# The gate of a projected piece: copy and tanh on ScalarE, the product later and in place on VectorE

## The chip, the cores and the metric

The kernel runs on one core of one Trainium2 chip. The metric is the device time of one execution in microseconds (us). Engine names are those of the profile: PE is TensorE's matmul, PEld its weight load, DVE is VectorE, ACT is ScalarE, POOL is GpSimd, SP is SyncE, which issues most DMAs.

## The reference, cut to what matters

A two-layer trunk of width 1024 runs for 1024 prompt tokens and for 8 samples of 4 tokens. Each layer normalizes, projects to 3592 columns, runs four token mixers side by side (S5, HGRN2, mLSTM, retention), gates each, and projects back:

```python
proj = jnp.einsum('bld,de->ble', h, w_in[l]).astype(f32)
...
hq = jax.nn.silu(to_heads(hg_q, HGRN_HEADS))
...
mixed = jnp.concatenate([s5_out * jax.nn.silu(s5_g), hg_out * jax.nn.silu(hg_g),
                         ml_out * jax.nn.silu(ml_g), rt_out * jax.nn.silu(rt_g)], axis=-1)
x = x + jnp.einsum('ble,ed->bld', mixed.astype(x.dtype), w_out[l])
```

The silu of a column g is computed as (tanh(g/2) + 1) * g, and the factor 2 that this leaves is taken out further on. Five of the projected blocks need it: `hg_q`, `hg_g`, the gate columns of `ml_ifg`, `rt_g` and `s5_g`.

## The kernel before, in words

The work runs in four passes n = 0 to 3: two layers, each as a first half of 512 prompt tokens and a second half of 512 prompt tokens with the 32 sample tokens. `make_plan` writes out one list of steps, and each engine walks the whole list in order and does its own part of each step. So the order on every engine is fixed, and an engine that waits holds up all that is behind it in its own queue.

A projection step ("mm", piece) lets PE multiply one piece of a block into one of three PSUM banks, which all pieces, the norm transposes and the out projection use in turn (`PB`, `bank_of`). "tok" blocks give pieces of 128 tokens x 256 columns (32 tokens in four groups of 64 columns for the samples); "ch" blocks (`hg_q`, `s5_g`) give pieces of 128 channels x 512 tokens on even passes and of 256 and 288 tokens on odd ones. Each matmul is done three times, with high and low parts of weights and activations. ACT makes the high part of a weight block (L1132), POOL the low part in eight pieces (L1088). A bank is free for the piece three places on when its `free` semaphore is raised, for which PE waits in `claim`.

The step ("take", piece) comes one piece after its "mm". For a gated piece (kind "av") ACT waits for the full bank and writes tanh(x/2) to one of two halves of the buffer `th` (L1218 and L1219 for "tok" pieces, L1221 for "ch" pieces; L1214 copies eight columns of `ml_ifg` aside first). DVE then multiplies: it reads the tanh from `th` and the piece from PSUM, writes the product to its place in SBUF (L1538 for `hg_q` into `hq`, L1545 for the three "tok" gates, L1548 for `s5_g` into `mixT`) and raises the bank's `free`. ACT's next tanh but one waits for that, since it writes the same half of `th`. `square_sum`, which makes the sums for the norms, uses `th` as scratch.

What lies around these steps, by line:

- L1989 to L2016 on DVE and L1403 to L1418 on ACT prepare one chunk of HGRN2 (steps A0, AX and A1). PE waits for the result at L2477. A0 of a pass's first chunk comes after the last `hg_g` piece.
- L1612, L1625 and L1635 on DVE set up the S5 parameters, woven in between the first pieces of pass 0. PE's L2299 and L2306 and ACT's L1306 and L1308 belong to the same set-up.
- L1904 and L1909 on DVE are the end of S5 of a pass (step z). The takes of the next pass's `hg_g` pieces come right behind it.
- L2402 on PE transposes the eight gate columns of mLSTM. It waits for the `free` of all `ml_ifg` pieces of its pass. ACT's L1380 to L1396 follow it.
- L2195 on DVE ends a chunk of any mixer; L2205 adds an out piece to the residual.

Of the kernel before, what the change touches and what calls it, by code (L numbers as in the profile page):

```python
# [351 lines left out]
def trunk_kernel(nc, inp, out, parts=("hg", "ml", "rt", "s5")):  # L352
    plan = make_plan(parts)
    ctx = ExitStack()
    with ctx:
# [3 lines left out]
        def signal(name, keys, unit=1):  # L359
            return Signal(nc, ctx, name, keys, unit)  # L360
# [249 lines left out]
        ud = nc.dram_tensor("ud", (256, W), F32, kind="Internal").ap()  # L610

        vexp = [QE.rearrange("p l a t -> p (l a t)")[0:TS, 768 + 512 * i:1280 + 512 * i] for i in range(2)]
        gate_of = {"hg": hgate, "rt": rgate, "ml": mgate}
        x1 = nc.dram_tensor("x1", (SEQ + TS, D), F32, kind="Internal").ap()
        x2 = nc.dram_tensor("x2", (SEQ + TS, D), F32, kind="Internal").ap()
# [41 lines left out]
        whi_done = signal("whi_done", in_blocks)  # L657
        wlo_done = signal("wlo_done", [b + (g,) for b in in_blocks for g in range(KT)])
        th_keys = [k for k in pieces if BLOCK[k[1]][4] == "av"]
        th_done = signal("th_done", th_keys)  # L660
        xo_in = [signal(f"xo_in{s}", [k for k in out_pieces if oslot[k] == s], 16) for s in range(3)]
        xo_sum = signal("xo_sum", out_pieces)
        xo_out = [signal(f"xo_out{s}", [k for k in out_pieces if oslot[k] == s], 16) for s in range(3)]
# [73 lines left out]
        def columns(key, lo, hi):  # L737
# [4 lines left out]
            cuts = [(g, max(lo, g * w), min(hi, (g + 1) * w)) for g in range(4)]  # L742
            return [(PB[bank_of[key]].t[TS * g:TS * g + TS, a - g * w:b - g * w], slice(a - lo, b - lo)) for g, a, b in cuts if a < b]

        def before(keys, key, back=1):
            i = keys.index(key)
            return keys[i - back] if i >= back else None

        def slot_before(k):
# [1 line left out]

        sums = [("final", t) if s[0] == "final" else (s[1], t) for s, t in plan if s[0] in ("prenorm", "final")]
        tables = [(s[1], part) if s[0] == "prenorm" else part[1] for s, part in plan
                  if s[0] == "prenorm" or s[0] == "proj" and part[0] == "take" and part[1] in th_done.value]

        def split_after(s, part):

# [10 lines left out]
        def levels(c):  # L768
            return LEVELS if c < NCH else SLEV
# [350 lines left out]
        def _(act):  # L1120
# [68 lines left out]
            def take_piece(k):  # L1189
# [12 lines left out]
                        act.wait_ge(*set_out.at(("s5set", 0, 10)))  # L1202
                act.wait_ge(*bank.full.at(k))
                if kind == "av":
                    i = th_keys.index(k)
                    last_sum = before(tables, k)
                    if last_sum in norm_tiles:
                        act.wait_ge(*ssq_done.at(last_sum))
                    if i >= 2:
                        act.wait_ge(*PB[bank_of[th_keys[i - 2]]].free.at(th_keys[i - 2]))  # L1210
                    v = th[:, i % 2, 0:ln]
                    if name == "ml_ifg":
                        act.wait_ge(*ml_clear.at(n))
                        nc.scalar.activation(ifc[0:ln, at, :], columns(k, 0, 8)[0][0], ACT.Copy).then_inc(*act_done.inc())  # L1214
                    if BLOCK[name][3] == "tok":
                        *some, last = columns(k, *((8, 264) if name == "ml_ifg" else (0, 256)))
                        for src, c in some:
                            nc.scalar.activation(th[0:ln, i % 2, c], src, ACT.Tanh, scale=0.5).then_inc(*act_done.inc())  # L1218
                        nc.scalar.activation(th[0:ln, i % 2, last[1]], last[0], ACT.Tanh, scale=0.5).then_inc(*th_done.inc(k))  # L1219
                        return  # L1220
                    nc.scalar.activation(v, ps, ACT.Tanh, scale=0.5).then_inc(*th_done.inc(k))  # L1221
                    return
                done = bank.free.inc(k)
                if name == "hg_f":
# [31 lines left out]

            for s, part in plan:
                if s[0] == "prenorm":
                    for k in [k for k in tables[:tables.index((s[1], part))] if k in th_done.value][-2:]:
                        act.wait_ge(*PB[bank_of[k]].free.at(k))  # L1260
                    square_sum((s[1], part))
                if s[0] == "norm":
                    n, t = s[1], part
# [133 lines left out]
                elif s in mixes and part == "AX":  # L1397
# [8 lines left out]
                    nc.scalar.activation(E[:, 8, 0:2 * T], chunk(hcum, c), ACT.Exp).then_inc(*hg_exp.inc(s))  # L1406
                    if c == 0:
                        Wn = HALF + TS * (n % 2)
                        for k in [k for k in pieces if k[:2] == (n, "hg_q")]:
                            act.wait_ge(*PB[bank_of[k]].free.at(k))  # L1410
                        past = [m for m in hg_mixes if m[1] < n]
                        if past:
                            act.wait_ge(*hg_prod.at(past[-1]))
                        if ("rt", n - 1, NCH) in samples:
                            act.wait_ge(*ss_new.at(("rt", n - 1, NCH)))
                        for par in range(2):
                            r = slice(par * 64, par * 64 + 64)
                            nc.scalar.activation(hq2[r, par, 0:2 * Wn], hq[r, 0:2 * Wn], ACT.Copy).then_inc(*(hg_pad.inc(n) if par else act_done.inc()))  # L1418
# [54 lines left out]
                                         aux.t[:, 0:256].rearrange("p (j t) -> p j t", j=2)[:, :, 0:T], ACT.Copy).then_inc(*aux.free.inc(mk_))  # L1473
                elif s[0] == "final":
                    if part == 0:
                        for k in [k for k in th_keys if k[0] == LAST and k[1][:2] in ("hg", "ml")][-2:]:
                            act.wait_ge(*PB[bank_of[k]].free.at(k))
                    for t in {0: (0, 1), NCH - 1: ()}.get(part, (part + 1,) if part < NCH else (part,)):
                        square_sum(("final", t))

# [2 lines left out]
        def _(dve):  # L1483
# [40 lines left out]
            def take_piece(k):  # L1524
# [4 lines left out]
                if kind == "a":  # L1529
                    return  # L1530
                if kind == "av":
                    dve.wait_ge(*th_done.at(k))
                    i = th_keys.index(k) % 2
                    if name == "hg_q":
                        v = th[:, i, 0:ln]
                        dsts = by_chunk(hq, k[2], at, ln)
                        for i, (dst, of) in enumerate(dsts):
                            nc.vector.scalar_tensor_tensor(dst, of(v), 1.0, of(ps), ALU.add, ALU.mult).then_inc(  # L1538
                                *(bank.free.inc(k) if i == len(dsts) - 1 else dve_done.inc()))
                        return  # L1540
                    if name == "s5_g":
                        v, dst = th[:, i, 0:ln], mixT[:, k[2], at:at + ln]
                    else:
                        for src, c in columns(k, *((8, 264) if name == "ml_ifg" else (0, 256))):
                            nc.vector.scalar_tensor_tensor(gate_of[name[:2]][0:ln, at, c], th[0:ln, i, c], 1.0, src, ALU.add, ALU.mult).then_inc(  # L1545
                                *(bank.free.inc(k) if c.stop == 256 else dve_done.inc()))
                        return
                    nc.vector.scalar_tensor_tensor(dst, v, 1.0, ps, ALU.add, ALU.mult).then_inc(*bank.free.inc(k))  # L1548
                    return

                dve.wait_ge(*bank.full.at(k))
# [21 lines left out]
            for s, part in plan:  # L1573
# [406 lines left out]
                elif s in mixes and part == "A0":  # L1980
                    n, c = s[1:]
                    T, cc = chunk_len(c), cols(c)
                    if c:
                        dve.wait_ge(*scores.full.at(("hg", n, c - 1, 0)))
                    for i, w in [*enumerate(levels(c)), (7, None)]:

                        blk, at = (2 * w, w) if w else ((CH if c < NCH else DSEQ),) * 2
                        x, e = (v.rearrange("p (m w) -> p m w", w=blk) for v in (chunk(hcum, c), E[:, i, 0:2 * T]))
                        nc.vector.tensor_tensor(e, x, x[:, :, at - 1:at].broadcast_to([P, 2 * T // blk, blk]), ALU.subtract).then_inc(  # L1989
                            *(dve_done.inc() if w else hg_diff.inc(s)))  # L1990
# [643 lines left out]
```

## Time and profile before

| what | value |
|---|---|
| median of 3 runs | 1601.3 us (1599.8 to 1604.67) |
| the profiled execution's own time | 1595.95 us |
| its span, first to last instruction | 1594.1 us |
| granted TensorE clock, mean | 0.923 |
| PE, DVE, ACT, POOL busy | 87%, 54%, 33%, 27% |

The span is what the rows of the profile add up to; the execution's own time is 1.85 us more than it. The median of the separate runs is 5.35 us above the profiled execution. Busy time counts an engine's instructions alone, so a wait shows as idle time in front of the instruction that ended it.

### The profile page before, as it was taken

The numbers are of one execution on the slowest core, as the hardware profiler recorded it, in microseconds if no ns is written. First come the engines' busy times: TensorE is split into PE (matmuls) and PEld (weight loads), VectorE is DVE, ScalarE is ACT, GpSimd is POOL, SyncE is SP. The second block draws the span as 40 slices with busy tenths as digits, with TensorE's granted clock in tenths as the row PEclk, the third lists the DMA queues.
The fourth block names the chain that finished last, engine by engine and source line by source line (L and its number), as shares of the span: only waits on it lengthen the run. The fifth ranks groups of instructions, "written<-read, shape, count | busy, mean of one in ns | idle before, by whom it ended". The sixth has DMA issues, their size and how long they took to land. (4 is left out here: it accounts for less than half of the span.)

```text
span 1594.1 us, 31551 instructions
## 1 busy us (share of the span) xinstructions
PE 1382.4 (87%) x12391; PEld 1210.3 (76%) x12391; DVE 865.9 (54%) x2652; ACT 524.2 (33%) x1093; POOL 436.3 (27%) x628
## 2 busy tenths in 40 slices
PE   2676899989897799898999989998989899889777
PEld 2565799778776788886777879877878799778546
DVE  4975736463795326455646442656465444644544
ACT  4344433333323423222433333333433432411011
POOL 4242343431002343231210244343200433331001
PEclk9798899989898899898999989998999998889879
DMA  6132123422233333362313423342213314449201
GB/s 172 64 109 67 53 82 107 139 86 81 67 108 105 97 91 82 93 103 71 109 63 97 127 67 108 107 139 80 94 57 114 100 56 121 148 72 193 64 9 57
DMA packets 167178, 149.83 MB, mean 94 GB/s; under 512 B 63440, under 2 KB 155352, under 8 KB 165240
## 3 DMA queue, kind: packets, MB, share of 16 engines
q1 hardware_dynamic: 96312, 76.38, 17.8%
q10 hardware_dynamic: 70720, 71.44, 15.6%
q8 instruction: 100, 1.64, 0.5%
q14 instruction: 46, 0.38, 0.1%
HBM read 124.42 MB, written 23.37 MB: 93 GB/s over the span
## 5 line engine op out<-in xcount | busy, mean ns | idle before, releaser
L1088 POOL TENSOR_TENSOR wlo<-wraw,whi 128x256 fp32r<-128x256 f32 (+1 forms) x448 | 339.3, 794 | 408.2 <-ACT whi L1132 408.2
L2280 PE MATMUL psum<-whi,hhi 128*128 128x256 f32 (+1 forms) x896 | 273.4, 305 | 36.3 <-DVE r L1545 20.5
L2280 PE MATMUL psum<-whi,hlo 128*128 128x256 f32 (+1 forms) x896 | 264.3, 295 | 0.0
L2280 PE MATMUL psum<-wlo,hhi 128*128 128x256 f32 (+1 forms) x896 | 263.7, 294 | 0.0
L2275 PE MATMUL psum<-hhi,whi 128*128 128x288 f32 (+2 forms) x672 | 232.4, 346 | 2.9 <-DVE hlo L1587 1.6
L2275 PE MATMUL psum<-hhi,wlo 128*128 128x288 f32 (+2 forms) x672 | 221.1, 329 | 0.0
L2275 PE MATMUL psum<-hlo,whi 128*128 128x288 f32 (+2 forms) x672 | 220.7, 328 | 0.0
L2280 PEld LDWEIGHTS psum<-whi,hhi 128*128 128x128 f32 x896 | 182.5, 204 | 44.7 <-issue 41.7
L1110 POOL TENSOR_SCALAR rs<-mv 128x4 f32<-128x4 f32 (+1 forms) x54 | 10.4, 193 | 634.1 <-DVE mv L2171 633.5
L2280 PEld LDWEIGHTS psum<-wlo,hhi 128*128 128x128 f32 x896 | 182.2, 203 | 0.7 <-issue 0.5
L2605 PE MATMUL psum<-wraw,mixT 128*128 128x256 f32 x768 | 178.5, 392 | 3.5 <-DVE xo L2205 3.5
L2280 PEld LDWEIGHTS psum<-whi,hlo 128*128 128x128 f32 x896 | 181.4, 202 | 0.0
L2605 PEld LDWEIGHTS psum<-wraw,mixT 128*128 128x128 f32 x768 | 149.3, 197 | 25.9 <-DVE xo L2205 4.4
L1132 ACT ACTIVATE whi<-wraw 128x2048 fp32r<-128x2048 f32 (+1 forms) x56 | 107.2, 1915 | 124.0 <-PE psum L2275 49.0
L2275 PEld LDWEIGHTS psum<-hhi,whi 128*128 128x128 f32 x672 | 130.0, 194 | 18.3 <-issue 6.7
L2275 PEld LDWEIGHTS psum<-hhi,wlo 128*128 128x128 f32 x672 | 130.4, 194 | 11.8 <-issue 3.0
L2275 PEld LDWEIGHTS psum<-hlo,whi 128*128 128x128 f32 x672 | 129.9, 193 | 10.3
L2168 DVE BATCH_NORM_STATS2 stats<-psum 128x6 f32<-128x64 f32 (+1 forms) x144 | 22.4, 217 | 104.3 <-PE psum L2526 104.2
L2526 PE MATMUL psum<-r,ST 128*128 128x64 f32 (+1 forms) x384 | 68.9, 283 | 1.1 <-issue 0.9
L1545 DVE SCALAR_TENSOR_TENSOR r<-th,psum 128x256 f32<-128x256 f32 (+3 forms) x72 | 24.9, 351 | 73.4 <-ACT th L1219 72.2
L1989 DVE TENSOR_TENSOR r<-r 128x256 f32<-128x256 f32 (+1 forms) x134 | 52.7, 464 | 17.7 <-PE psum L2437 17.6
L2526 PEld LDWEIGHTS psum<-r,ST 128*128 128x128 f32 x384 | 57.5, 200 | 2.6 <-issue 2.4
(351 smaller groups left out, 2253.9 us busy)
## 6 DMA issues: line engine op xcount, KB each, us to landing
wraw<-in_w_in ACTq DMA_DIRECT2D x50, 1024.0 KB, 5.3
wraw<-in_w_out ACTq DMA_DIRECT2D x14, 1024.0 KB, 5.4
x<-xo SPq DMA_DIRECT2D x48, 128.0 KB, 2.3
r<-x SPq DMA_DIRECT2D x10, 512.0 KB, 5.5
r<-in_c_rot SPq DMA_DIRECT2D x4, 1088.0 KB, 8.0
wraw<-in_w_in ACTq DMA_DIRECT2D x4, 1056.0 KB
r<-WTm SPq DMA_DIRECT2D x4, 1024.0 KB, 11.4
r<-VTm SPq DMA_DIRECT2D x4, 1024.0 KB, 5.4
```

The costliest lines, as they stand in the source:

```text
L1088: nc.gpsimd.tensor_tensor(wlo[:, hslot[b], ks, 0:width], wraw[:, wslot[b], ks, 0:width], whi[:, hslot[b], ks, 0:width].bitcast(F32), ALU.s ...
L1110: nc.gpsimd.tensor_scalar(rs[0:T, :], mv[0:T, :, 1], EPS if s[0] == "rt" else 4 * EPS, 4.0, ALU.add, ALU.mult).then_inc(*pool_done.inc())
L1132: nc.scalar.activation(whi[:, hslot[b], :, 0:width], wraw[:, wslot[b], :, 0:width], ACT.Copy).then_inc(*whi_done.inc(b))
L1545: nc.vector.scalar_tensor_tensor(gate_of[name[:2]][0:ln, at, c], th[0:ln, i, c], 1.0, src, ALU.add, ALU.mult).then_inc(*(bank.free.inc(k) ...
L1989: nc.vector.tensor_tensor(e, x, x[:, :, at - 1:at].broadcast_to([P, 2 * T // blk, blk]), ALU.subtract).then_inc(*(dve_done.inc() if w else ...
L2168: nc.vector.bn_stats(stats[0:T, h, :], src[:, h, :]).then_inc(*dve_done.inc())
L2275: mm = nc.tensor.matmul(bank.t[:, 0:c.stop - c.start], w[:, sl, kt, k[2] * P:(k[2] + 1) * P], x[:, kt, c], start=first, stop=last)
L2280: mm = nc.tensor.matmul(bank.t[:, 0:width], x[:, kt, c], w[:, sl, kt, 0:width], start=first, stop=last)
L2526: mm = nc.tensor.matmul(o, stt[0:T, h, 0:T], v(h), start=br == "ml", stop=True)
L2605: mm = nc.tensor.matmul(bank.t[0:r, 0:256], mixT[:, row, k[2] * P:k[2] * P + r], wraw[:, wslot[b], kt, 0:256], start=kt == 0, stop=kt == 7)
```

## The change

For a gated piece ACT now first copies the piece from PSUM to its final place (`hq`, the gate buffer or `mixT`), then writes the tanh to a ring in `th`, and raises the bank's `free` itself. DVE waits for that `free`, and makes the product in place from two SBUF operands, the tanh of the ring and the copied piece; it raises a new semaphore, `gated`. The ring `th_flat` has 1024 columns, given out in order: a "tok" piece takes 256 of them, a "ch" piece 512 or 288. ACT waits before a tanh for the `gated` of the latest earlier piece whose columns it overwrites. With "tok" pieces one after the other that is the fourth piece back, where before it was the second. For the sample tokens DVE makes one product of 32 x 256 in place of four of 32 x 64. `hg_q` pieces that span the prompt and the samples are split in two for ACT too.

The diff, cut to its core:

```diff
+        th_flat = th.rearrange("p a x -> p (a x)")
...
-        th_done = signal("th_done", th_keys)
+        gated = signal("gated", th_keys)
+        th_at, th_last = {}, {}
+        for k in th_keys:
+            w = 256 if BLOCK[k[1]][3] == "tok" else HALF if k[0] % 2 == 0 else W - HALF // 2
+            lo = th_at[before_key][1] if th_at else 0
+            lo = lo if lo + w <= 2 * HALF else 0
+            over = [q for q in th_at if th_at[q][0] < lo + w and lo < th_at[q][1]]
+            th_last[k] = over[-1] if over else None
+            th_at[k], before_key = (lo, lo + w), k
...
+        def gate_moves(k, ps, at, ln):
+            name, lo = k[1], th_at[k][0]
+            if BLOCK[name][3] == "tok":
+                return [(src, gate_of[name[:2]][0:ln, at, c], th_flat[0:ln, lo + c.start:lo + c.stop])
+                        for src, c in columns(k, *((8, 264) if name == "ml_ifg" else (0, 256)))]
+            v = th_flat[:, lo:lo + ln]
+            if name == "hg_q":
+                return [(of(ps), dst, of(v)) for dst, of in by_chunk(hq, k[2], at, ln)]
+            return [(ps, mixT[:, k[2], at:at + ln], v)]
...
@@ take_piece of ScalarE
                 if kind == "av":
-                    i = th_keys.index(k)
-                    last_sum = before(tables, k)
-                    if last_sum in norm_tiles:
-                        act.wait_ge(*ssq_done.at(last_sum))
-                    if i >= 2:
-                        act.wait_ge(*PB[bank_of[th_keys[i - 2]]].free.at(th_keys[i - 2]))
-                    v = th[:, i % 2, 0:ln]
+                    sums_before = [q for q in tables[:tables.index(k)] if q in norm_tiles]
+                    if sums_before:
+                        act.wait_ge(*ssq_done.at(sums_before[-1]))
                     if name == "ml_ifg":
                         act.wait_ge(*ml_clear.at(n))
                         nc.scalar.activation(ifc[0:ln, at, :], columns(k, 0, 8)[0][0], ACT.Copy).then_inc(*act_done.inc())
-                    if BLOCK[name][3] == "tok":
-                        *some, last = columns(k, *((8, 264) if name == "ml_ifg" else (0, 256)))
-                        for src, c in some:
-                            nc.scalar.activation(th[0:ln, i % 2, c], src, ACT.Tanh, scale=0.5).then_inc(*act_done.inc())
-                        nc.scalar.activation(th[0:ln, i % 2, last[1]], last[0], ACT.Tanh, scale=0.5).then_inc(*th_done.inc(k))
-                        return
-                    nc.scalar.activation(v, ps, ACT.Tanh, scale=0.5).then_inc(*th_done.inc(k))
+                    moves = gate_moves(k, ps, at, ln)
+                    for src, dst, _ in moves:
+                        nc.scalar.activation(dst, src, ACT.Copy).then_inc(*act_done.inc())
+                    if th_last[k] is not None:
+                        act.wait_ge(*gated.at(th_last[k]))
+                    for src, _, t in moves[:-1]:
+                        nc.scalar.activation(t, src, ACT.Tanh, scale=0.5).then_inc(*act_done.inc())
+                    src, _, t = moves[-1]
+                    nc.scalar.activation(t, src, ACT.Tanh, scale=0.5).then_inc(*bank.free.inc(k))
                     return
...
@@ take_piece of VectorE
                 if kind == "av":
-                    dve.wait_ge(*th_done.at(k))
...
-                            nc.vector.scalar_tensor_tensor(dst, of(v), 1.0, of(ps), ALU.add, ALU.mult).then_inc(
-                                *(bank.free.inc(k) if i == len(dsts) - 1 else dve_done.inc()))
...
-                    nc.vector.scalar_tensor_tensor(dst, v, 1.0, ps, ALU.add, ALU.mult).then_inc(*bank.free.inc(k))
+                    dve.wait_ge(*bank.free.at(k))
+                    if BLOCK[name][3] == "tok":
+                        dst, lo = gate_of[name[:2]][0:ln, at, :], th_at[k][0]
+                        nc.vector.scalar_tensor_tensor(dst, th_flat[0:ln, lo:lo + 256], 1.0, dst, ALU.add, ALU.mult).then_inc(*gated.inc(k))
+                        return
+                    moves = gate_moves(k, ps, at, ln)
+                    for i, (_, dst, v) in enumerate(moves):
+                        nc.vector.scalar_tensor_tensor(dst, v, 1.0, dst, ALU.add, ALU.mult).then_inc(*(gated.inc(k) if i == len(moves) - 1 else dve_done.inc()))
                     return
...
@@ ScalarE, before square_sum of a prenorm step (the same edit before the final norm and in AX for hg_q)
-                    for k in [k for k in tables[:tables.index((s[1], part))] if k in th_done.value][-2:]:
-                        act.wait_ge(*PB[bank_of[k]].free.at(k))
+                    for k in [k for k in tables[:tables.index((s[1], part))] if k in th_keys][-1:]:
+                        act.wait_ge(*gated.at(k))
...
@@ VectorE, step A0 of hg
                     if c:
                         dve.wait_ge(*scores.full.at(("hg", n, c - 1, 0)))
+                    else:
+                        dve.wait_ge(*gated.at(last_piece[(n, "hg_q")]))
```

## Rows read from the trace of the kernel before

**Rows 1.** Page, part 1: busy us, share of the span and instructions of each engine
```profile
PE 1382.4 (87%) x12391; PEld 1210.3 (76%) x12391; DVE 865.9 (54%) x2652; ACT 524.2 (33%) x1093; POOL 436.3 (27%) x628
```

**Rows 2.** Waits of PE: line waited for, us in total, times, longest us
```profile
PE psum L2280 <- DVE r L1545: 20.5, 6, 8.0
...
PE psum L2402 <- DVE r L1545: 10.1, 3, 8.3
...
PE psum L2275 <- DVE r L1545: 1.2, 1, 1.2
PE psum L2280 <- DVE r L1538: 1.1, 1, 1.1
...
PE psum L2299 <- DVE r L1545: 0.5, 1, 0.5
```

**Rows 3.** Answer for line L1545: durations in ns, min/median/max, and forms
```profile
L1545 DVE SCALAR_TENSOR_TENSOR r<-th,psum x72: 202/416/422, 96.2 to 1424.2; 128x256 f32<-128x256 f32 x48, 32x64 f32<-32x64 f32 x16, 32x66 f32<-32x66 f32 x6, 32x58 f32<-32x58 f32 x2
```

**Rows 4.** Timeline of ACT, 395 to 398: start us, us, instruction, idle before
```profile
395.77 0.68 ACT L1218 ACTIVATE th<-psum 32x64 f32<-32x64 f32 x3
396.48 0.63 ACT L1219 ACTIVATE th<-psum 32x64 f32<-32x64 f32 x2
```

**Rows 5.** Timeline of DVE in the same stretch
```profile
397.25 2.08 DVE L1909 SCALAR_TENSOR_TENSOR mixT<-r,mixT 128x512 f32<-128x512 f32 x2
399.37 0.20 DVE L1545 SCALAR_TENSOR_TENSOR r<-th,psum 32x64 f32<-32x64 f32 x1
```

**Rows 6.** Timeline of PE, restarts after a wait, in five windows
```profile
400.46 0.36 PE L2280 MATMUL psum<-whi,hhi 128*128 128x256 f32 x1 [2.86 <-DVE r L1545]
...
821.19 0.36 PE L2280 MATMUL psum<-whi,hhi 128*128 128x256 f32 x1 [2.00 <-DVE r L1545]
...
1158.50 0.36 PE L2280 MATMUL psum<-whi,hhi 128*128 128x256 f32 x1 [2.86 <-DVE r L1545]
...
544.03 1.03 PE L2402 MATMUL psum<-const,r 128*4 128x128 f32 x8 [0.72 <-DVE r L1545]
...
155.65 0.58 PE L2402 MATMUL psum<-const,r 128*4 128x128 f32 x2 [8.28 <-DVE r L1545]
```

**Rows 7.** Timeline of ACT around 816, 541 and 155
```profile
816.57 0.68 ACT L1219 ACTIVATE th<-psum 128x256 f32<-128x256 f32 x2
...
540.09 0.38 ACT L1219 ACTIVATE th<-psum 128x256 f32<-128x256 f32 x1
...
154.68 0.38 ACT L1219 ACTIVATE th<-psum 128x256 f32<-128x256 f32 x1
```

**Rows 8.** Groups of ACT by line and shape: busy us, mean ns, idle before
```profile
L1219 ACT ACTIVATE th<-psum 128x256 f32<-128x256 f32 x48 | 18.2, 384 | 86.9 <-PE psum L2280 70.1 <-DVE r L1545 13.4 <-DVE r L1538 3.4
...
L1218 ACT ACTIVATE th<-psum 32x64 f32<-32x64 f32 x12 | 2.5, 210 | 0.2
```

**Rows 9.** Durations of two DVE lines whose inputs both lie in SBUF
```profile
L1989 DVE TENSOR_TENSOR r<-r x134: 219/419/961, 103.6 to 1262.4; 128x256 f32<-128x256 f32 x128, 128x64 f32<-128x64 f32 x6
...
L2195 DVE TENSOR_TENSOR y<-y,rs x54: 412/426/861, 143.5 to 1521.9; 128x256 f32<-128x256 f32 x48, 32x256 f32<-32x256 f32 x6
```

**Rows 10.** Timeline of DVE and POOL, 131 to 138, then DVE at 441
```profile
131.85 0.42 DVE L1545 SCALAR_TENSOR_TENSOR r<-th,psum 128x256 f32<-128x256 f32 x1 [3.50 <-ACT th L1219]
...
132.85 4.75 DVE L2002 TENSOR_TENSOR r<-r 128x128 f32<-128x128 f32 x7
...
131.49 5.97 POOL L1088 TENSOR_TENSOR wlo<-wraw,whi 128x256 fp32r<-128x256 f32 x8 [31.11 <-ACT whi L1132]
...
441.26 1.50 DVE L2002 TENSOR_TENSOR r<-r 128x128 f32<-128x128 f32 x7
```

**Rows 11.** Timeline of DVE, 95 to 103, and of PE at 113
```profile
95.61 0.69 DVE L1538 SCALAR_TENSOR_TENSOR r<-th,psum 128x512 f32<-128x512 f32 x1
...
102.29 0.42 DVE L1545 SCALAR_TENSOR_TENSOR r<-th,psum 128x256 f32<-128x256 f32 x1
...
113.30 1.04 PE L2306 MATMUL psum<-r 64*16 64x128 f32 x8 [6.13 <-ACT r L1308]
```

More of the change, by code:

```diff
@@ L753, in trunk_kernel @@
         tables = [(s[1], part) if s[0] == "prenorm" else part[1] for s, part in plan
-                  if s[0] == "prenorm" or s[0] == "proj" and part[0] == "take" and part[1] in th_done.value]
+                  if s[0] == "prenorm" or s[0] == "proj" and part[0] == "take" and part[1] in th_keys]
         def split_after(s, part):
@@ L1408, in _ @@
                         Wn = HALF + TS * (n % 2)
-                        for k in [k for k in pieces if k[:2] == (n, "hg_q")]:
-                            act.wait_ge(*PB[bank_of[k]].free.at(k))
+                        act.wait_ge(*gated.at(last_piece[(n, "hg_q")]))
                         past = [m for m in hg_mixes if m[1] < n]
@@ L1475, in _ @@
                     if part == 0:
-                        for k in [k for k in th_keys if k[0] == LAST and k[1][:2] in ("hg", "ml")][-2:]:
-                            act.wait_ge(*PB[bank_of[k]].free.at(k))
+                        act.wait_ge(*gated.at([k for k in th_keys if k[0] == LAST and k[1][:2] in ("hg", "ml")][-1]))
                     for t in {0: (0, 1), NCH - 1: ()}.get(part, (part + 1,) if part < NCH else (part,)):
@@ L1531, in take_piece @@
                 if kind == "av":
-                    dve.wait_ge(*th_done.at(k))
[L1533 to L1537, printed above, removed]
-                            nc.vector.scalar_tensor_tensor(dst, of(v), 1.0, of(ps), ALU.add, ALU.mult).then_inc(
-                                *(bank.free.inc(k) if i == len(dsts) - 1 else dve_done.inc()))
-                        return
[L1541 to L1547, printed above, removed]
-                    nc.vector.scalar_tensor_tensor(dst, v, 1.0, ps, ALU.add, ALU.mult).then_inc(*bank.free.inc(k))
+                    dve.wait_ge(*bank.free.at(k))
+                    if BLOCK[name][3] == "tok":
+                        dst, lo = gate_of[name[:2]][0:ln, at, :], th_at[k][0]
+                        nc.vector.scalar_tensor_tensor(dst, th_flat[0:ln, lo:lo + 256], 1.0, dst, ALU.add, ALU.mult).then_inc(*gated.inc(k))
+                        return
+                    moves = gate_moves(k, ps, at, ln)
+                    for i, (_, dst, v) in enumerate(moves):
+                        nc.vector.scalar_tensor_tensor(dst, v, 1.0, dst, ALU.add, ALU.mult).then_inc(*(gated.inc(k) if i == len(moves) - 1 else dve_done.inc()))
                     return
```

## The prediction, made blind

> **What bounds the kernel now.** I read the busy times first. PE is busy for 87% of the span, 1382.4 of 1594.1 us, and no other engine comes near [rows 1]. So 212 us are left, and a change to ACT and DVE can only pay through the waits of PE. I read these next, by what ended them. The gated product ends twelve of them, 33.4 us together: 20.5 in front of L2280, 10.1 in front of L2402, and three small groups of 1.2, 1.1 and 0.5 [rows 2]. The change takes DVE out of exactly this release. The product itself is short, at most 422 ns [rows 3]. So where a bank is free late, that is either because the product stood in DVE's queue behind other work, or because ACT's tanh was late already. The timelines in front of each wait tell which. The reader is to see in them two patterns: one in which ACT has long finished and DVE is still busy elsewhere, and one in which ACT starts its tanh less than 1 us before PE restarts.
>
> **The gain: banks that DVE frees late.** The clearest place is the start of pass 1. ACT writes the tanhs of the sample piece from 395.77 on (four of 32 x 64), and the next piece's right behind [rows 4]. DVE is in S5's last step until 399.33 and makes the products from 399.37 on [rows 5]. PE restarts at 400.46 after 2.86 us [rows 6], so it had been ready at 397.60. After the change the bank is free after four copies and four tanhs on ACT. Three small ones back to back take 0.68 us with a mean of 0.21 each, so a further one costs 0.235 us, and eight take about 1.9: free at 397.7. The gain is 2.6, with some 0.15 for the semaphore. Pass 3 repeats the picture at 1158.50 with the same 2.86 [rows 6]: 2.6 again. At pass 2 two tanhs of full pieces start at 816.57 and take 0.68 together [rows 7], so a copy or tanh behind another costs 0.30; the first bank is free at 817.3 by then, and PE, ready at 819.19, loses its whole wait of 2.00 [rows 6]. The wait of 0.72 at 544.03 [rows 6] goes too: its tanh started at 540.09, and tanh plus copy are over by 540.8 [rows 7]. Sum: 2.6 + 2.6 + 2.0 + 0.7 = 7.9 us. These four carry through, because what comes after them, the last piece, the first HGRN2 chunk behind it and PE's work, moves forward with PE.
>
> **Waits that stay, because ACT is late.** In front of 155.65 PE waits 8.28 us, the longest of the twelve [rows 6]. There the tanh starts only at 154.68 [rows 7], since ACT has come through a chunk's exponentials and a weight block. A copy of 0.30 takes the place of a product of 0.42, so this wait shrinks by about 0.15 at most. The waits at 529.36 (7.97), 916.41 (3.46) and 1269.10 (1.12), all of them parts of the sums in [rows 2], look the same: ACT starts the tanh 0.9 to 2.1 us before PE restarts. These four are 20.8 of the 33.4 us.
>
> **Waits whose gain is swallowed.** Those of 1.06 at 96.44, 1.18 at 144.35 and 1.33 at 1262.00, parts of [rows 2] too, are ended by DVE's queue, and the bank will be free in time. But PE then reaches a later wait earlier whose end DVE and ACT set on their own: 113.30 (6.13 us, [rows 11]), 155.65 and 1269.10. I count 0 for them and keep their 3.6 us for the range; the twelfth wait, 0.5 at L2299, belongs to the S5 set-up and ends with it either way. Something small comes with them: in pass 0 the last `hg_g` tanh waited for DVE, and now it doesn't, so the HGRN2 chunk behind it starts 0.3 earlier.
>
> **The cost on ACT.** There are 96 tanhs before (54 on L1219, 18 on L1218, 24 on L1221). After, each of the five blocks is copied once more and `hg_q` is split four times: 100 copies and 4 more tanhs. A full piece's tanh takes 384 ns alone, a small one 210 [rows 8]. With 72 full and 28 small ones the copies add some 28 + 6 = 34 us to ACT's 524.2 [rows 1], most of it in idle time. What of it lies on a path to PE: 0.30 for the copy of the last `hg_g` piece in passes 1, 2 and 3, since the first HGRN2 chunk starts with it (0.9 in all); 0.30 at 131.4, where DVE waits for an `ml_ifg` tanh and 155.65 hangs on what it does next [rows 10]; and 0.6 for two such in pass 3 in front of 1269.10, less 0.15 each at 155.65 and 1269.10. Together 1.5. Were the other copies hidden nowhere, the cost would be 34; were all hidden, 0. I take 0 for them, because PE's three banks give each piece two pieces' time, about 5.6 us, in which ACT has to find 0.68.
>
> ACT's new wait for the ring costs nothing. By the layout of the 1024 columns it is for the second piece back at the closest, as before, with one exception: the first `hg_q` of pass 2, which waits for the piece just before it, an `s5_g` made long ago.
>
> **The cost on DVE.** 18 instructions fewer, since the sample pieces take one product in place of four: some 3 us of DVE's time, off PE's paths. The product's inputs now both lie in SBUF. The trace before doesn't show this very instruction, but it shows its neighbours. The old product, with one input in PSUM, never took over 422 ns [rows 3], whatever POOL did. DVE's L1989 and L2195, of the same 256 columns with both inputs in SBUF, have medians of 419 and 426 but reach 961 and 861 [rows 9]. The long ones are those that run while POOL writes `wlo`. The plainest case: seven L2002 take 4.75 us beside POOL's burst of 131 to 137, and 1.50 us at 441 without it [rows 10]. So a product that falls into a burst costs about 961 − 419 = 0.54 more, one outside it nothing. Laid instruction by instruction beside POOL's timeline, 33 of the old product's 100 ran beside a burst. Four of them lie on a path to PE: the two `hg_q` products of pass 0 at 89.5 and 95.6, the `hg_g` one behind (DVE is busy without a break there until the product at 102.29, and the wait at 113.30 hangs on it [rows 11]), and the one at 131.85 [rows 10]. 4 × 0.54 = 2.2. The bounds: 0, if the stretching needs a burst in another phase, and 33 × 0.54 = 17.8.
>
> The Trainium skill, page "SBUF — State Buffer", section "Who interferes with whom", says that a VectorE instruction with two SBUF inputs contends with a GpSimd instruction that reads SBUF, that the lock is exclusive, and that the later one blocks for the whole of the other; with one SBUF input there is no contention. The trace agrees so far: 961 against 422 at most. By it POOL's `wlo` is held up by each product as well, and the first matmul of the next block with it, which speaks against this change.
>
> **The sum.** −7.9 − 0.3 + 1.5 + 2.2 = −4.5 us. Against the profiled execution, 1595.95, that is 1591.4. The median of the runs shown is 5.35 above, so 1601.3 − 4.5 = 1596.8.
>
> **Rivals.**
> 1. *More comes out* (0.25). The swallowed 3.6 us come back because the DVE chain in front of them gets shorter too, and products miss the bursts: −7.9 − 3.6 − 0.3 + 1.5 = −10.3, 1591. For it: 33.4 us of waits are ended by this instruction. Against: at 113.30 and 155.65 PE waits for other things.
> 2. *ACT takes it back* (0.17). The copies sit in front of HGRN2's exponentials and the mixers' evacuations, which end many waits of PE. Fifteen more of the 100 on such a path at 0.30 give 4.5 back: 1601. Then the change doesn't do what it says: the banks are no earlier where it matters.
> 3. *Slower: products against POOL's bursts* (0.13). DVE's and POOL's long instructions take turns. Each of the 33 costs DVE 0.54 and POOL up to 0.42. The gain without this term is 6.7 us, so it is slower by over 0.3% from 11.5 us or 21 of the 33 on; with 21 on paths 1606. For it: it is plain in the trace that these two stretch each other. Against: I find only four on a path.
>
> **How the numbers follow.** Forecast 0.45, by itself 1593 to 1601; rivals 0.25, 0.17 and 0.13. Under 0.3%, 4.8 us here, a measurement of this kernel hardly tells a change from none. The forecast lies just inside that: I give 0.19 of its 0.45 to faster and 0.26 to the same. Faster: 0.19 + 0.24 of rival 1 = 0.43. Same: 0.26 + 0.01 + 0.15 of rival 2 = 0.42. Slower: 0.02 + 0.13 = 0.15. The range goes from rival 1 to rival 3: 1590 to 1606.
>
> **What would show it.** In the profile after, PE's waits before the `hg_g` pieces at the start of passes 1, 2 and 3 should be gone or below 0.3, and the wait of L2402 in pass 0 should still be near 8, now ended by ACT. ACT should be near 558 us busy. The product's median should stay near 419, with a maximum near 960; if that stays at 422, the 2.2 is wrong. The prediction fails if a wait in front of L2477 or L2402 grows by more than 1 us, if POOL's `wlo` gets slow enough that PE waits for it, or if weight loads land later.

## The result and the profile after

The kernel after the change takes 1594.33 us (median of 12 runs, 1588.86 to 1599.51); the kernel before takes 1601.11 beside it (12 runs, 1598.33 to 1605.12). The ratio of the runs is 0.9949 with a 95% interval of 0.9934 to 0.9964. That is 8.2 us faster, between 5.8 and 10.6. The profiled execution after took 1594.12 us with a span of 1592.3, close to its median. The one before lies 5 us below its median, so the two traces differ by only 1.8 us. Times of whole kernels are therefore compared by their runs, and the traces are used for places.

Page of the kernel after, part 1, against [rows 1]:

```profile
PE 1383.3 (87%) x12391; PEld 1210.4 (76%) x12391; DVE 865.7 (54%) x2634; ACT 551.6 (35%) x1197; POOL 443.7 (28%) x628
```

ACT grew by 27.4 us (34 were expected), DVE did not move. The waits of PE that ACT's tanh of a gated piece now ends, in the kernel after, against [rows 2] (us in total, times, longest):

```profile
PE psum L2411 <- ACT th L1239: 11.9, 2, 9.0
PE psum L2289 <- ACT th L1239: 11.8, 4, 6.5
```

33.4 us in twelve waits have become 23.7 in six, but 3.6 at 103.84 are new, in the S5 set-up of pass 0. Timeline of PE after, restarts of PE in six windows, against [rows 6]:

```profile
399.08 0.36 PE L2289 MATMUL psum<-whi,hhi 128*128 128x256 f32 x1 [0.19 <-ACT th L1239]
...
1153.73 0.36 PE L2289 MATMUL psum<-whi,hhi 128*128 128x256 f32 x1 [0.19 <-ACT th L1239]
...
157.21 0.80 PE L2411 MATMUL psum<-const,r 128*4 128x128 f32 x3 [8.98 <-ACT th L1239]
...
526.70 0.56 PE L2289 MATMUL psum<-whi,hhi 128*128 128x264 f32 x1 [6.47 <-ACT th L1239]
...
912.98 0.56 PE L2289 MATMUL psum<-whi,hhi 128*128 128x264 f32 x1 [4.92 <-ACT th L1239]
...
1264.08 0.58 PE L2411 MATMUL psum<-const,r 128*4 128x128 f32 x2 [2.92 <-ACT th L1239]
```

The two of 2.86 are down to 0.19, and those of 2.00 and 0.72 are gone. Timelines of ACT and DVE after, 397 to 401, against [rows 4] and [rows 5]:

```profile
397.06 0.92 ACT L1233 ACTIVATE r<-psum 32x64 f32<-32x64 f32 x4
398.00 0.69 ACT L1237 ACTIVATE th<-psum 32x64 f32<-32x64 f32 x3
398.72 0.22 ACT L1239 ACTIVATE th<-psum 32x64 f32<-32x64 f32 x1
```

```profile
398.54 2.32 DVE L1916 SCALAR_TENSOR_TENSOR mixT<-r,mixT 128x512 f32<-128x512 f32 x2
```

Eight small instructions take 1.88 us on ACT, and PE restarts 0.14 after the last. DVE is in S5's last step until 400.86, and nobody waits for it there.

One thing more went with a wait. Busy times by window (us of the window; PE, PEld, DVE, ACT, POOL busy; PEclk, the granted clock, as a share of 2.4 GHz; DMA share; GB/s), the restart at the start of pass 2, first in the kernel before, then after:

```profile
821.00:828.00 7.00, 6.81 (x36) 6.56 (x37) 2.56 (x9) 0.77 (x2) 0.00 (x0) 0.76 0.00 0
```

```profile
816.00:823.00 7.00, 7.00 (x53) 6.74 (x52) 6.05 (x15) 1.97 (x7) 0.00 (x0) 1.00 0.00 0
```

Behind its 2.00 us wait PE was granted 0.76 over 7 us, as much as 3.4 us at the lower level, 1.2 GHz (7 × 0.24 × 2). Without the wait it stayed at 2.4 GHz. That is worth 7 × 0.24 = 1.7 us: with the matmuls of the two traces matched by their numbers, the kernel after moved 3.7 us forward at this place, not 2.0.

The two longer waits of 2.86 us had no such price. The same table for the kernel before, behind each of them:

```profile
400.00:407.00 7.00, 6.54 (x52) 6.49 (x53) 1.72 (x6) 1.16 (x3) 0.00 (x0) 1.00 0.43 75
1158.00:1165.00 7.00, 6.50 (x52) 6.46 (x53) 1.72 (x6) 1.16 (x3) 0.00 (x0) 1.00 0.01 2
```

The granted clock was 1.00 behind both, and the matmuls moved forward there by the idle time alone, 2.7 us each. Over the whole execution the granted clock is 0.923 in both traces, so the kernel after lost elsewhere what it won at pass 2. Over the twelve runs of the kernel after it averages 0.922, over the runs of the kernel before beside the experiments 0.919, 0.920 and 0.921.

### The profile page after: what moved, and what is told of

The parts are those of the page before. It is cut to its first block, busy times and chain, and to the rows that moved or that the text cites. A ratio compares the mean times of both kernels' runs of the same rounds, so it can differ in the third digit from the quotient of the medians.

```text
span 1592.3 us, 31632 instructions
## 1 busy us (share of the span) xinstructions
PE 1383.3 (87%) x12391; PEld 1210.4 (76%) x12391; DVE 865.7 (54%) x2634; ACT 551.6 (35%) x1197; POOL 443.7 (28%) x628
## 4 chain that ended last, share of the span: by engine, by line
PE 60%; DVE 18%; ACT 7%; DMA 6%; issue 5%; POOL 3%; SPq 1%; DVEq 0%; ACTq 0%; POOLq 0%
PE psum L2289 16%; PE psum L2284 15%; PE psum L2614 5%; DVE r L1619 3%; PE psum L2592 3%; DVE r L1998 2%; PE psum L2535 2%; DMA wraw<-in_w_in 2%; PE psum L2534 1%; ACT r L1421 1%; PE psum L2356 1%; POOL rs L1133 1%; PE psum L2446 1%; DVE QE L2019 1%; PE psum L2532 1%
## 5 line engine op out<-in xcount | busy, mean ns | idle before, releaser
L1108 POOL TENSOR_TENSOR wlo<-wraw,whi 128x256 fp32r<-128x256 f32 (+1 forms) x448 | 346.9, 810 | 412.8 <-ACT whi L1152 412.8
L2284 PEld LDWEIGHTS psum<-hhi,wlo 128*128 128x128 f32 x672 | 130.0, 193 | 11.8 <-issue 3.0
L2284 PEld LDWEIGHTS psum<-hlo,whi 128*128 128x128 f32 x672 | 129.3, 192 | 10.3
L1551 DVE SCALAR_TENSOR_TENSOR r<-th,r 128x256 f32<-128x256 f32 (+1 forms) x54 | 25.0, 479 | 73.5 <-ACT th L1239 73.3
```

The source lines that it names most:

```text
L1108: nc.gpsimd.tensor_tensor(wlo[:, hslot[b], ks, 0:width], wraw[:, wslot[b], ks, 0:width], whi[:, hslot[b], ks, 0:width].bitcast(F32), ALU.s ...
L1551: nc.vector.scalar_tensor_tensor(dst, th_flat[0:ln, lo:lo + 256], 1.0, dst, ALU.add, ALU.mult).then_inc(*gated.inc(k))
L2284: mm = nc.tensor.matmul(bank.t[:, 0:c.stop - c.start], w[:, sl, kt, k[2] * P:(k[2] + 1) * P], x[:, kt, c], start=first, stop=last)
```

## The experiments

All kernels ran in five rounds beside the kernel before. The edit of e2 is against e1, those of e7 and of e9 to e12 are against e6, and all others against the kernel after. "Theory" and "rival" are those of the expectation above each measurement. The microseconds are (ratio − 1) × 1601.1, the figures in brackets their 95% intervals. The intervals of a difference of two ratios add as squares.

**e1: the deeper ring alone.** The tanh goes to the ring, but DVE still multiplies out of PSUM and frees the bank.

```diff
-dve.wait_ge(*bank.free.at(k))
-nc.vector.scalar_tensor_tensor(dst, v, 1.0, dst, ALU.add, ALU.mult).then_inc(*gated...)
+dve.wait_ge(*th_done.at(k))
+nc.vector.scalar_tensor_tensor(dst, v, 1.0, src, ALU.add, ALU.mult).then_inc(*bank.free...)
```

> The deeper ring for the tanhs alone: ACT makes no copy, DVE's product reads PSUM and frees the bank, as before. The prediction's theory (banks are freed late because DVE stands in step z of S5): nothing changes at those places, since the bank still waits for DVE; 0 us, ratio 0.999 to 1.001. Rival (ACT was held by the two-slot buffer, 17 us of waits, and the ring is what pays): 5 to 8 us faster, ratio 0.995 to 0.997.

Measured: 0.9987 (0.9972 to 1.0003), −2 us (−4.5 to +0.5). The rival's 5 to 8 us are excluded: the ring is not what pays.

**e2: e1 with the copies too**, on ACT ahead of each tanh, and read by nobody before DVE overwrites them.

```diff
+for src, dst, _ in moves:
+    nc.scalar.activation(dst, src, ACT.Copy).then_inc(*act_done.inc())
```

> The copies without their use: ring and products as in the first kernel, but ACT also copies every gated piece to its final place ahead of its tanh, and DVE's product (still from PSUM) overwrites it. The prediction's theory: only the copies on a path to PE cost, 1.5 us, and every one of them delays the tanh and so DVE's release: 1.5 to 3 us slower than before, ratio 1.001 to 1.002. Rival (ACT's load is on the path in many places): 4.5 us or more slower, ratio 1.003 and up.

Measured: 1.0044 (1.003 to 1.0057), +7 us; against e1 +9 (6 to 12). The rival's number came out, and the prediction's 1.001 to 1.002 is excluded: the copies are not free where DVE still frees the bank. Most of it has a place. Timelines of PE, 694 to 716, in e1 and then in e2:

```profile
712.57 0.40 PE L2298 MATMUL psum<-hlo,whi 128*128 128x288 f32 x1 [1.86 <-issue]
```

```profile
710.86 0.61 PE L2298 MATMUL psum<-hlo,whi 128*128 128x288 f32 x1 [5.15 <-issue]
```

This stall of PE stands in the middle of a block and is ended by nothing that the profile shows. It is 3.3 us longer in e2, and the granted clock behind it was 0.52 from 711 to 716. Matched by their numbers, the matmuls of e2 fall back by 5.5 us against e1 at this place, and by 2.2 more up to 750. The stall is in e1 too, which has no copies, and in e4 (2.66), but in none of the other traces, so copies are not needed for it. The 16 DMA engines were full at the time (share 1.09 from 705 to 711 in e2); what PE waits for is not shown. So e2 shows what the copies cost, but not that ACT's load is the reason.

**e3 and e4: the change in two parts.** `NEW` picks the pieces that take the new way; the others keep DVE's product out of PSUM. e3 has it for the 14 `hg_g` pieces of passes 1 to 3 only, e4 for all the others only.

```diff
-NEW = lambda k: True
+NEW = lambda k: k[1] == "hg_g" and k[0] > 0           # e3
+NEW = lambda k: not (k[1] == "hg_g" and k[0] > 0)     # e4
```

> The change for the 14 hg_g pieces of passes 1 to 3 alone, all others as before (with the ring). The prediction's theory: these carry the waits of 2.86, 2.00 and 2.86 us, so 7.2 - 0.9 = 6.3 us faster than before, ratio 0.996, as good as the whole change. Rival (the gain is spread over all 78 pieces, or comes from the chunk steps): about a fifth of it, 1 to 2 us.

> The complement: the change for all pieces but these 14. The prediction's theory: -0.7 (L2402 in pass 1) - 0.3 + 0.6 (copies) + 2.2 (products beside POOL in pass 0) = 1.8 us slower than before, ratio 1.001, and PE waits about 2.9, 2.0 and 2.9 us again at the starts of passes 1 to 3. Rival: 4 to 6 us faster.

Measured: e3 0.9941 (0.9926 to 0.9956), −9.4 us, more than its theory's 6.3; e4 0.9996 (0.9981 to 1.0011), −0.6. Both rivals are excluded. The parts add up to −10.0 (± 3.4), the whole gave −8.2. The gain is the one piece type at the start of three passes; for all the rest the change does nothing measurable.

**e5: the product left out.** As the kernel after, but DVE makes statistics of the tanh (one input, in SBUF) in place of the product, so the gates stay ungated.

```diff
-nc.vector.scalar_tensor_tensor(dst, th_flat[0:ln, lo:lo + 256], 1.0, dst, ALU.add, ALU.mult)
+nc.vector.bn_stats(dst[:, 0:6], th_flat[0:ln, lo:lo + 256])
```

> The whole change, but the product left out: in its place DVE takes statistics of the tanhs in the ring (one input in SBUF, six columns out), so the gates stay the ungated copies. Same instruction count, same waits, about the same DVE time, but no second SBUF input. Theory (products in place are stretched beside POOL's bursts, 2.2 us of it on PE's path): 2 us faster than the whole change, ratio to before 0.9935, and no such instruction beside a burst is longer than one outside. Rival (the stretching is off the path): the same as the whole change, 0.995.

Measured: 0.9928 (0.9914 to 0.9942), 3.4 us less than the kernel after (± 3.3). Durations in ns, min/median/max, of the product in the kernel after, then of what stands in its place in e5:

```profile
L1551 DVE SCALAR_TENSOR_TENSOR r<-th,r x54: 404/424/979, 98.1 to 1422.1; 128x256 f32<-128x256 f32 x48, 32x256 f32<-32x256 f32 x6
L1555 DVE SCALAR_TENSOR_TENSOR r<-th,r x16: 185/422/1132, 90.0 to 1146.1; 128x256 f32<-128x256 f32 x8, 128x512 f32<-128x512 f32 x4, 128x32 f32<-128x32 f32 x4
```

```profile
L1565 DVE BATCH_NORM_STATS2 r<-th x54: 397/423/431, 96.7 to 1418.9; 128x6 f32<-128x256 f32 x48, 32x6 f32<-32x256 f32 x6
```

With two inputs in SBUF the same columns take up to 979 ns, with one never over 431. The stretching that the prediction took from its neighbours is real. The Trainium skill, page "SBUF — State Buffer", section "Who interferes with whom", lets a VectorE instruction with two SBUF inputs and a GpSimd one that reads SBUF exclude each other, and a one-input instruction run free; these durations agree. On the other side, L1108 on POOL has a median of 736 ns after against 737 before, but its longest went from 2.4 to 5.1 us. That one is in the burst in front of pass 3's first HGRN2 chunk. Timelines of POOL and DVE there, of the kernel before, then of the kernel after:

```profile
1248.86 5.89 POOL L1088 TENSOR_TENSOR wlo<-wraw,whi 128x256 fp32r<-128x256 f32 x8 [5.38 <-ACT whi L1132]
1250.90 4.20 DVE L2002 TENSOR_TENSOR r<-r 128x128 f32<-128x128 f32 x7
```

```profile
1244.12 10.34 POOL L1108 TENSOR_TENSOR wlo<-wraw,whi 128x256 fp32r<-128x256 f32 x8 [5.02 <-ACT whi L1152]
1246.49 1.49 DVE L2011 TENSOR_TENSOR r<-r 128x128 f32<-128x128 f32 x7
```

Before, DVE's seven instructions with two SBUF inputs were stretched to 4.20 us. After, they took 1.49, as they do without POOL at 441 in the kernel before, and POOL's eight took 4.45 us longer. So at this place POOL is the one that is held up. It is not the product that does it: e5, without the product, has one of 4.9 us there too, while e3, e7, e8 and e12 have none over 2.4. It goes with when the two bursts meet.

**e6: the copy frees the bank.** The tanh reads the copied piece in SBUF, so PE no longer waits for it. ACT waits for its own copy before the tanh, and DVE waits for the tanh.

```diff
-nc.scalar.activation(dst, src, ACT.Copy).then_inc(*act_done.inc())
+nc.scalar.activation(dst, src, ACT.Copy).then_inc(*bank.free.inc(k))       # the last one of a piece
...
-nc.scalar.activation(t, src, ACT.Tanh, scale=0.5).then_inc(*bank.free.inc(k))
+nc.scalar.activation(t, dst, ACT.Tanh, scale=0.5).then_inc(*th_done.inc(k))
```

> The whole change with the bank freed by the copy alone; ACT's tanh then reads the copy in SBUF. Theory (where ACT is late, the bank follows ACT's queue): each of the waits near 157, 527, 913 and 1264 us, and the rests of 0.2 near 399 and 1154, shrinks by the tanh's 0.3 to 0.4 or by four small ones' 0.9: 2 us faster than the whole change, ratio 0.9935. Rival (what the copies cost lies in ACT's own queue, not in the bank): no difference from the whole change, 0.995.

Measured: 0.9905 (0.9888 to 0.9922), −15.2 us. With e9 it is the fastest kernel that computes the gate, and faster than its own theory's 0.9935, which the interval excludes. Timelines of e6, PE's restarts at three places, and ACT at the first:

```profile
523.84 0.56 PE L2305 MATMUL psum<-whi,hhi 128*128 128x264 f32 x1 [4.88 <-ACT r L1242]
...
905.88 0.36 PE L2305 MATMUL psum<-whi,hhi 128*128 128x264 f32 x1 [3.19 <-ACT r L1242]
...
155.26 0.37 PE L2427 MATMUL psum<-const,r 128*4 128x128 f32 x1 [7.49 <-ACT r L1242]
```

```profile
522.78 0.92 ACT L1242 ACTIVATE r<-psum 32x58 f32<-32x58 f32 x4
523.73 0.55 ACT L1248 ACTIVATE th<-r 32x58 f32<-32x58 f32 x3
524.18 0.24 ACT L1250 ACTIVATE th<-r 32x66 f32<-32x66 f32 x1
```

PE restarts 1.06 us after the start of ACT's first copy, when the four tanhs have just begun. In the kernel after ACT began the same copies at 524.67 and PE came at 526.70, 2.03 later. The two rests of 0.19 are gone too. The direct saving over the kernel after is 0.97 here, 0.28 at each of three full pieces (copy to restart 0.80 after, 0.52 in e6) and 0.38 for the rests: 2.2 us. The runs say 7.0 (± 3.6). So between 1 and 8 us more came than the five places explain. In the two traces, matched by their matmuls, e6 gains 8.1 us on the kernel after, and 3.9 of them lie between 1340 and 1440, where the kernel after gives time back (see below). By one execution each that is where the largest part of the rest comes from.

**e7: the early release for `hg_g` of passes 1 to 3 alone**, the edit of e6 and this one:

```diff
-NEW = lambda k: True
+NEW = lambda k: k[1] == "hg_g" and k[0] > 0
```

> The change for the 14 hg_g pieces of passes 1 to 3, with the bank freed by the copy. Theory: as the third experiment (0.9941) with another 0.2 to 0.3 us at each pass's start: 0.9935 to 0.994. Rival (the tanh reading SBUF, or the extra wait between copy and tanh, costs as much as it gives): 0.9945 or more.

Measured: 0.9943 (0.9923 to 0.9963), no different from e3. At those places 0.4 us of the release was left to gain, too little to tell its theory from its rival.

**e8: the change in pass 0 alone**, with the bank freed by the tanh.

```diff
-NEW = lambda k: True
+NEW = lambda k: k[0] == 0
```

> The change in pass 0 alone. The prediction's theory: no wait of PE of this pass is gained, the copies and three stretched products cost: 2.2 - 0.3 + 0.15 = 2 us slower, ratio 1.001, PE at its matmul 500 some 1.5 to 2 us later than before. Rival (pass 0 gains its 1.06, 0.5 and 1.18 us): 2 to 3 us faster.

Measured: 1.0006 (0.9993 to 1.002), +1 us (−1 to +3). Its wait in front of the transpose of the gate columns is 9.0, ended by ACT. The rival's gain of 2 to 3 us is excluded: in pass 0 nothing is to be had.

**e9, e10 and e11: where the early release pays.** All three have the edit of e6.

```diff
-NEW = lambda k: True
+NEW = lambda k: k[0] > 0                                       # e9
+NEW = lambda k: k[1] in ("hg_g", "ml_ifg") and k[0] > 0        # e10
+NEW = lambda k: not (k[1] == "hg_g" and k[0] > 0)              # e11
```

> The bank is released by ACT's copy, and the tanh reads the copy in SBUF, for all gated pieces of passes 1, 2 and 3; pass 0 is as in the kernel before. With the release by the copy in every pass the ratio to the kernel before was 0.9905, 15 us. Theory A: the 7 us that it has over the changed kernel come from the waits where ACT is late, which each lose the tanh's time (8.98 to 7.49 in pass 0, 6.47 to 4.88 in pass 1, 4.92 to 3.19 in pass 2), and pass 0 holds 1.5 to 2 us of them. Then this run gives -13 us, a ratio near 0.992. Rival B: what the early release mends is the loss of the change in pass 0 (the changed kernel stands 1.5 us behind there, this one 0.2 ahead) and little else; then most of the 7 us is gone and the ratio is that of the whole change, 0.995.

> Release by the copy for hg_g and ml_ifg of passes 1 to 3 alone, 42 of the 96 pieces; the others as in the kernel before. Theory A: the pieces on which PE waits in these passes are hg_g at the start of a pass and ml_ifg in front of the transpose of the gate columns (6.47 at 526.70, 4.92 at 912.98, 2.92 at 1264.08), so these two blocks hold nearly all: a ratio near 0.992, the same as with all pieces of passes 1 to 3. Rival B: hg_g alone carries it, and ml_ifg adds nothing; then 0.994, as measured with hg_g alone.

> Release by the copy for all gated pieces but hg_g of passes 1 to 3, which stay as in the kernel before. Freed by the tanh, the same set gave 0.9996. Freed by the copy, hg_g of passes 1 to 3 alone gave 0.9943, no more than its 0.9941 with the tanh. Theory A: so the 7 us of the early release must come from this set: 0.9996 - 0.0044 = 0.995. Rival B: the early release pays only together, since PE that comes earlier out of one place waits at the next; then this run stays near 0.999.

Measured: e9 0.9908 (0.989 to 0.9926), −14.7 us; e10 0.9928 (0.991 to 0.9945), −11.5; e11 0.9986 (0.997 to 1.0001), −2.2. e9 is as fast as e6, so theory A holds in that passes 1 to 3 carry all that can be measured; rival B's 0.995 is excluded. The 1.5 to 2 us that theory A allowed for pass 0 can't be read from e6 less e9 (0.5 ± 4.0). e10 lies between its theories, neither excluded. e11 came out at its rival's number: with `hg_g` as before, the early release of all the others gives 2.2 us, where its theory A had 8. In passes 1 to 3 they give 5.6 once `hg_g` has it too (e9 less e7, ± 4.3). An earlier PE that meets the next bank earlier would look like that, but the two differ by less than their scatter.

**e12: e6 with the product left out**, in the way of e5.

> Release by the copy in all passes, and the product left out: DVE makes bn_stats of the tanh in its place, with one input in SBUF, so the gates stay ungated. Against the whole change the same replacement gave 3.4 us, which I put down to the products with two SBUF inputs beside POOL's bursts. Theory A: that cost does not depend on who frees the bank, so it adds to the 15 us: a ratio near 0.9885. Rival B: it came from the product's place in DVE's queue in front of the release of work on the path at 155 and 113 us, which the early release has already mended; then 0.9905, as with the product.

Measured: 0.9904 (0.9885 to 0.9923), against 0.9905 for e6 with its product. The rival's number came out, and theory A's lies at the end of the interval: once the copy frees the bank, the product costs PE 0.2 us (± 4.1). Why it is so, by its place in DVE's queue or because e5's 3.4 us were within the scatter, these runs don't tell.

## Why the prediction was right, and where its sizes were off

The direction and the mechanism were right: 1596.8 was predicted for a median of 1594.33. The waits at the four places named went, and e3 shows that three of them, the starts of passes 1 to 3, carry the gain. The predicted gain of 4.5 us is below the measured 8.2 and outside its interval of 5.8 to 10.6. Two sizes were off the same way: the gain was too small by the clock at pass 2, and the cost on DVE has no place on PE's path that the runs show. That the gains of the sum alone, 7.9 + 0.3, give the measured 8.2 is luck: by the traces more than that was gained, and part of it given back later.

**The gain: banks that DVE frees late, 7.9.** By the traces 2.67 + 2.67 + 2.00 + 0.72 = 8.1 of waits went. The reading was exact, down to the 1.9 us for eight small instructions on ACT (1.88). What was too small is what one of them is worth: "These four carry through" priced the idle time alone, as if PE ran at one clock. At 821.19 the lower clock behind the wait went as well, 1.7 us; at 400.46 and 1158.50 there was none to win. In e3, which holds just the three places at the starts of passes, the matmuls move forward by 2.7, 3.8 and 2.7 us, and give back 0.28 at each when the first HGRN2 chunk is reached, which is the 0.30 that the prediction put for the copy. That leaves 8.3 us; the runs give 9.4 (7.0 to 11.8), the prediction had 6.3.

**Waits that stay, because ACT is late.** Right: the four are there, ended by ACT, and 8.28 became 8.98. The "0.15 at most" is not how they move. 7.97 became 6.47, and 3.46 became 4.92. Timelines of ACT after, the weight blocks in front of the second and the third:

```profile
521.72 1.91 ACT L1152 ACTIVATE whi<-wraw 128x2048 fp32r<-128x2048 f32 x1 [7.40 <-DMA wraw<-in_w_in]
...
910.17 1.91 ACT L1152 ACTIVATE whi<-wraw 128x2048 fp32r<-128x2048 f32 x1 [3.47 <-DMA wraw<-in_w_in]
```

ACT is late there because a weight block lands late. It issued the load of the first at 513.02 and could use the block 8.70 later, in the kernel before 9.93 after the issue at 514.38. For the second it was 6.80 after and 5.63 before. So the two waits moved by −1.5 and +1.5 us, and 1.2 us of each is the time of a transfer. "Weight loads land later" was one of the prediction's signs of failing: it is seen at the second of these places, not at the first.

**Waits whose gain is swallowed, 0 of 3.6.** Held. Those at 96.44, 144.35 and 1262.00 are gone, and e8 puts pass 0 at +1 us. The wait at 1269.10 grew from 1.12 to 2.92 as the 1.33 in front of it went. That is more than the 1 us which the prediction named as a sign of failing for L2402. The granted clock behind it was 0.76 over 7 us, where it had been 1.00, another 1.7 us: at this place the kernel after loses more than it had won.

**The cost on ACT, 1.5.** The 0.9 in it for the last `hg_g` copies is seen in e3, 0.28 three times. "I take 0 for them" held the other copies to be hidden, and that was too easy: e2 shows that copies alone cost 9 us (6 to 12) while DVE frees the bank. In the change their place and the earlier release come together: e4 puts the other 82 pieces, copies, products and all, at −0.6 (−3.0 to +1.8), where the sum had −0.7 − 0.3 + 0.6 + 2.2 = +1.8 for them.

**The cost on DVE, 2.2.** The mechanism is shown (979 ns against 431), the price on PE's path is not. e5 gives 3.4 ± 3.3, e12 against e6 0.2 ± 4.1. Rival 3 asked for 21 of the 33 on a path; at 0.54 each that is 11.3 us, and both runs exclude it. POOL, which that page of the Trainium skill has held up by DVE, kept its median, and the one burst that took 4.45 us longer agrees with the page. It did not reach PE through `wlo`: PE waits for it in eight places with 2.6 us in all, before 2.7.

**The rivals.** Rival 1's total, −10.3, is nearer to the measured 8.2 than the forecast and inside the interval. Half of its reason is wrong, since the swallowed 3.6 us did not come back; the other half, that the products cost PE nothing, is not excluded (e12). The result excludes rivals 2 and 3.

**What is given back behind the gain.** In the traces matched matmul by matmul, the kernel after is 6.2 us ahead at 1338 and 2.1 ahead at 1472. Lines of the timelines there, of the kernel after, then of e9, in which nothing is given back (11.4 and 10.9 ahead):

```profile
1379.79 0.32 SPq L843 DMA_DIRECT2D r<-x  x1
1383.24 1.06 ACT L1191 ACTIVATE th<-r 128x1024 f32<-128x1024 f32 x1 [3.46 <-issue]
1385.40 1.28 DVE L1537 SCALAR_TENSOR_TENSOR r<-r,rstd 128x1024 f32<-128x1024 f32 x1 [3.50 <-POOL rstd L1119]
1393.88 0.66 PE L2573 MATMUL psum<-const,y 128*128 128x128 f32 x2 [5.10 <-ACT kT L1470]
```

```profile
1373.41 0.32 SPq L851 DMA_DIRECT2D r<-x  x1
1376.85 1.06 ACT L1199 ACTIVATE th<-r 128x1024 f32<-128x1024 f32 x1 [2.16 <-issue]
1379.01 1.28 DVE L1547 SCALAR_TENSOR_TENSOR r<-r,rstd 128x1024 f32<-128x1024 f32 x1 [2.21 <-POOL rstd L1127]
1387.66 0.66 PE L2589 MATMUL psum<-const,y 128*128 128x128 f32 x2 [3.99 <-ACT kT L1480]
```

A row tile of `x` is loaded, ACT sums its squares 3.45 us later, and DVE scales it, 1.28 us, in the queue of the mLSTM chunk on which PE waits. In e9 that instruction is over at 1380.29, just before the chunk's first one at 1380.38. In the kernel after it sits in front of it, and PE's wait is 5.10 for 3.99. That is 1.1 of the 4.1 us. Another 1.3 are the next wait, 3.39 at 1413.60 for 2.05 in the kernel before, and 1.7 the granted clock from 1409 to 1421, 0.72 for 0.86. e5 and e10 give back 4 us at the same place, e7 3, e3 1. That this hangs on an issue about 1 us later or earlier in SP's queue is argued from traces of one execution each, and no run moved that load.

## What to carry to other kernels

Find out which engine is late at each wait before taking another out of the release: here 8.1 of 33.4 us were to be had from DVE, and 20.8 belonged to ACT and its transfers. Then release a bank after the first instruction that no longer needs it, not the last: the copy, not the tanh. It pays only where PE comes to that bank: 14 of 96 pieces carried the gain of the change. And look at the granted clock behind a wait before pricing it: at one of three waits here it nearly doubled the gain, at the two longer ones it added nothing.

## What the runs showed of the hardware

**A short wait can cost clock, and need not.** In the kernel before, the granted clock was 0.76 over the 7 us behind the wait of 2.00 at 821.19, which costs 1.7 us, nearly as much as the wait itself. Behind the waits of 2.86 at 400.46 and 1158.50 it was 1.00. So neither the length of a wait nor its presence alone tells the price; the rows behind it do.

**Either of two engines can be the one that is held up.** VectorE instructions with two SBUF inputs beside GpSimd's `wlo` took 4.20 us for seven at 1250.90 in the kernel before; in the kernel after the seven took 1.49, and GpSimd's eight 10.34 instead of 5.89.

**One trace has a scatter of its own.** e7 and e10 have the same instructions in pass 0. Timelines of PE in e7 and in e10, the same matmul:

```profile
96.16 0.36 PE L2305 MATMUL psum<-whi,hhi 128*128 128x256 f32 x1 [0.94 <-DVE r L1562]
```

```profile
97.07 0.55 PE L2305 MATMUL psum<-whi,hhi 128*128 128x256 f32 x1 [2.62 <-DVE r L1562]
```

Matmul 500 starts at 118.42 in the one and at 122.50 in the other. All fourteen traces together tell more than a pair. Six of the seven kernels with the change in pass 0 have a wait of 2.5 to 3.6 us near 103, as the new 3.62 of the kernel after, and none of the seven without it has one there. So the place of this wait comes with the change. But its time does not show: matmul 500 starts at 120.7 on average with the change in pass 0, and at 120.4 without it (119.2 to 122.3 and 118.4 to 122.7).

**The tanh out of SBUF** takes 418 ns for 128x256 in e6 and in e10. Out of PSUM it takes 394 in the kernel after and 383 in e10, which has both. Reading the copy costs ACT 24 to 35 ns a piece.
